# Four layer norms with an early half mean: squares summed under the last units, a new order in first units, and later tiles moved by 256 bytes

## What is computed

```
def layer_norm(x, g, b):
    mu = mean(x); var = mean(square(x - mu))
    return (x - mu) * rsqrt(var + 1e-5) * g + b

for i in range(2):
    h = layer_norm(ALPHA * h + mixer(h), ln_mix_g[i], ln_mix_b[i])
    h = layer_norm(ALPHA * h + square(relu(h @ w_up)) @ w_down, ln_mlp_g[i], ln_mlp_b[i])
```

## Time and profile before

| What | Value |
|---|---|
| runs | 1338.17, 1333.67, 1337.58 us; median 1337.58 |
| the profiled execution | 1333.9 us, its span from first to last instruction 1332.1 us |
| TensorE busy | 1283.2 us, 96% of the span |
| VectorE busy | 888.7 us, 67% |
| ScalarE busy | 642.5 us, 48% |
| mean granted TensorE clock | 0.989 |
| weights and other data read | 196.08 MB, 148 GB/s over the span |

### The profile page before, as it was taken

One profiled execution on the slowest core, in us unless ns is written; L12 is line 12 of the kernel. 1 busy time (PEld: TensorE's weight loads), 2 busy tenths in 40 slices (PEclk: granted clock), 3 DMA queues, 4 the chain that ended last, 5 costly groups with the idle time before them and its releaser, 6 DMA issues.

```text
span 1332.1 us, 25095 instructions
## 1 busy us (share of the span) xinstructions
PE 1283.2 (96%) x10634; PEld 1245.3 (93%) x10634; DVE 888.7 (67%) x1374; ACT 642.5 (48%) x834; POOL 46.3 (3%) x40
## 2 busy tenths in 40 slices
PE   9989999999987999999999999999999999999997
PEld 8868999999987999999999999899998989999997
DVE  6875764565568567646565459899766655899843
ACT  5464453443453335435435444554454454777631
POOL 0561000000000000000000000000000000000000
PEclk9999999999998999999999999999999999999999
DMA  9222255455331134554533543334454241454430
GB/s 358 97 107 95 98 190 202 175 189 189 130 127 64 64 127 156 192 190 163 204 111 128 189 163 129 144 138 168 149 187 168 94 154 64 158 185 173 177 128 32
DMA packets 28505, 198.41 MB, mean 149 GB/s; under 512 B 3440, under 2 KB 3952, under 8 KB 4736
## 3 DMA queue, kind: packets, MB, share of 16 engines
q1 hardware_dynamic: 27792, 195.83, 40.5%
q10 hardware_dynamic: 624, 1.31, 0.3%
HBM read 196.08 MB, written 1.05 MB: 148 GB/s over the span
## 4 chain that ended last, share of the span: by engine, by line
PE 79%; DVE 11%; ACT 4%; issue 2%; DMA 2%; POOL 2%; DVEq 0%; ACTq 0%
PE lin L462 23%; PE lin L464 23%; PE lin L463 23%; DVE wlo L1471 3%; PE lin L544 3%; PE att L537 2%; DVE conv L1950 2%; DMA raw<-units_dram 2%; ACT whi L1029 1%; PE lin L567 1%; POOL pr L447 1%; DVE qk L1812 1%; DVE z L1562 0%; POOL lg L447 0%; DVE h L1568 0%
## 5 line engine op out<-in xcount | busy, mean ns | idle before, releaser
L462 PE MATMUL lin<-xh,whi 128*128 128x256 f32 x1936 | 555.7, 287 | 3.9 <-DVE xl L1525 2.1
L1471 DVE TENSOR_TENSOR wlo<-raw,whi 128x2048 fp32r<-128x2048 f32 x179 | 409.6, 2291 | 212.3 <-ACT whi L1029 211.6
L463 PE MATMUL lin<-xl,whi 128*128 128x256 f32 x1936 | 549.8, 284 | 0.0
L464 PE MATMUL lin<-xh,wlo 128*128 128x256 f32 x1936 | 549.5, 284 | 0.0
L1029 ACT ACTIVATE whi<-raw 128x2048 fp32r<-128x2048 f32 x183 | 348.6, 1907 | 180.6 <-PE lin L464 167.3
L462 PEld LDWEIGHTS lin<-xh,whi 128*128 128x128 f32 x1936 | 373.5, 193 | 8.7 <-issue 5.5
L463 PEld LDWEIGHTS lin<-xl,whi 128*128 128x128 f32 x1936 | 373.6, 193 | 0.6 <-issue 0.5
L464 PEld LDWEIGHTS lin<-xh,wlo 128*128 128x128 f32 x1936 | 373.4, 193 | 0.0
L462 PE MATMUL lin<-fh,whi 128*128 128x256 f32 x512 | 143.4, 280 | 0.0
L463 PE MATMUL lin<-fl,whi 128*128 128x256 f32 x512 | 142.8, 279 | 0.0
L464 PE MATMUL lin<-fh,wlo 128*128 128x256 f32 x512 | 142.8, 279 | 0.0
(11 more groups left out here) (336 smaller groups left out, 1600.9 us busy)
## 6 DMA issues: line engine op xcount, KB each, us to landing
raw<-units_dram SPq DMA_DIRECT2D x183, 1024.0 KB, 4.8
h<-x_dram SPq DMA_DIRECT2D x1, 1024.0 KB, 6.9
memT<-mem_dram ACTq DMA_DIRECT2D x1, 1024.0 KB, 4.8
out_dram<-h SPq DMA_DIRECT2D x4, 256.0 KB, 2.0
consts<-consts_dram SPq DMA_DIRECT2D x1, 864.0 KB, 15.6
narrow_a<-narrow_a_dram SPq DMA_DIRECT2D x1, 544.0 KB, 8.7
vec<-vectors_dram SPq DMA_DIRECT2D x1, 245.5 KB, 17.8
posi<-pos_dram SPq DMA_DIRECT2D x1, 128.0 KB, 8.6
```

What stands on the lines that cost most here:

```text
L462: mm(out, w[0], a[0], start=first, stop=False)
L463: mm(out, w[0], a[1], start=False, stop=False)
L464: return mm(out, w[1], a[0], start=False, stop=last)
L1471: v.tensor_tensor(wlo[u % RING][:], raw[u % RING][:], whi[u % RING][:].bitcast(f32), ALU.subtract).then_inc(lo_ready, 1)
```

## The change

- **The early mean.** In the middle of unit 2 of 4 (narrow) or 4 of 8 (wide) TensorE multiplies the sum of the first four blocks by ones (`near_sum`, a job of its own). VectorE subtracts an eightfold share of that from all blocks (`near_shift`): from the two pairs that are done, from the two pairs that are still to come by way of the residual, and from zsum. From then on the blocks lie around a value near the mean.
- **Squares under the last units.** ScalarE squares each block as soon as it is done (`near_squares`), VectorE adds the squares up (`add_squares`), the last unit of a narrow group becomes two jobs of one block each. After the last block one tile of squares is left for TensorE to sum. The true variance is that sum less the square of the remaining mean: ScalarE squares the mean's row of one partition (shsq), TensorE adds it with a factor of -1 (a new constant, neg).
- **The norm.** VectorE waits for that square, centres two pairs, takes the reciprocal, and centres the other two, the third with a wait for its end. zsum is cleared after h.
- **`unit_first`** does the two products with xh of a pair first and the one with xl a pair later, at all eleven places.
- **Keep-warm matmuls**: in `norm` 2 instead of 4 ahead of `spread`; in `layer_norm` 1, 2 and 8 instead of 6, 4 and 11.
- **Loops.** The second half of the down projections is written out instead of looped.
- **Place.** An unused tile of 224 bytes per partition behind xl, and 8 more columns of constants, put consts 224 bytes and all tiles behind it 256 bytes higher.

```diff
+                def with_high(c):
+                    pe.wait_ge(split_hi, SPLIT[event] + c + 1)
+                    for m in range(2):
+                        for k in (2 * c, 2 * c + 1):
+                            w = tile(u, m * DB + k)
+                            mm(o[:, m, :], w[0], xh[:, k, :], start=m == k == 0, stop=False)
+                            mm(o[:, m, :], w[1], xh[:, k, :], start=False, stop=False)
...
+                with_high(0)
+                for c in range(1, 4):
+                    with_high(c)
+                    with_low(c - 1)
+                with_low(3).then_inc(job_done, 1)
...
+            def near_sum(ln):
+
+                pe.wait_ge(z_summed, SUMMED[ln] + 4)
+                mm(bank(JOB[ln + "_shift", 0])[:, 0, :], ones, zsum[:], start=True, stop=True).then_inc(job_done, 1)
...
             def norm(name, idle=6):
                 keep_warm(idle)
                 square_sum(name)
-                keep_warm(4)
+                keep_warm(2)
                 spread(name)
                 keep_warm(11)
...
                 mm(bank(JOB[name + "_mean", 0])[:, 0, :], ones, zsum[:], start=True, stop=True).then_inc(job_done, 1)
-                norm(name)
+                pe.wait_ge(near_added, ADDED[name] + 5)
+                o = bank(JOB[name + "_sq", 0])
+                token_sum(o, 0, squares_of[0][:, 0, :], True, False)
+                keep_warm(1)
+                pe.wait_ge(shift_squared, LN[name] + 1)
+                flat = o[:].rearrange("p a s -> p (a s)")
+                for t in range(2):
+                    last = mm(flat[:, t * P:t * P + 8], shsq[:, t * P:(t + 1) * P], const("neg")[0:1, :], start=False, stop=t == 1)
+                last.then_inc(job_done, 1)
+                keep_warm(2)
+                spread(name)
+                keep_warm(8)
...
             def layer_norm(name, event, bias):
-                squares(name, z, is_centered(name))
+
+                j = JOB[name + "_mean", 0]
+                filled(act, j)
+                f(shsq, lin[j % RING][0:1, 0, :], ACT.Square, scale=D ** -0.5).then_inc(shift_squared, 1)
...
+            def narrow_units(name, ln):
+
+                for i in range(4):
+                    high_part(U0[name] + i + AHEAD)
+                    if i == 3:
+                        near_squares(ln, is_shifted(ln, 0), (0, 1))
+                        near_squares(ln, is_shifted(ln, 1), (2, 3))
+                        near_squares(ln, lambda: evacuated(act, JOB[name, 2]), (4, 5))
+                near_squares(ln, lambda: evacuated(act, JOB[name, 3]), (6,))
+                near_squares(ln, lambda: evacuated(act, JOB[name, 3] + 1), (7,))
...
-                center(name, z, D)
-                inverse(name)
-                link(v.memset(zsum[:], 0.0))
-                is_centered(name)
+                j = JOB[name + "_mean", 0]
+                p = psum(j)
+                dve.wait_ge(shift_squared, LN[name] + 1)
+                for c in range(4):
+                    ins = v.scalar_tensor_tensor(out=two(z, c), in0=over(p[:, 0, :]), scalar=-1.0 / D, in1=two(z, c), op0=ALU.mult, op1=ALU.add)
+                    if c == 3:
+                        read_out(ins, j)
+                    elif c == 1:
+                        inverse(name)
+                    elif c == 2:
+                        link(ins)
+                evacuated(dve, j)
...
+            def near_shift(ln, src, alpha):
+
+
+                j = JOB[ln + "_shift", 0]
+                p = psum(j)
+                for n, c in enumerate((2, 3, 0, 1)):
+                    v.scalar_tensor_tensor(out=two(z, c), in0=over(p[:, 0, :]), scalar=-2.0 / D / (alpha if c >= 2 else 1.0),
+                                           in1=two(src if c >= 2 else z, c), op0=ALU.mult, op1=ALU.add).then_inc(shifted, 1)
+                read_out(v.scalar_tensor_tensor(out=zsum[:], in0=p[:, 0, :], scalar=-8.0 / D, in1=zsum[:], op0=ALU.mult, op1=ALU.add), j)
+                evacuated(dve, j)
+                dve.wait_ge(shifted, 4 * LN[ln] + 4)
...
                 for i in range(4):
                     low_part(U0[name] + i + AHEAD)
                     j = JOB[name, i]
...
+                    if i == 2:
+                        near_shift(ln, h, ALPHA)
+                    elif i == 3:
+                        add_squares(ln, 1, 2, sq[0][:], sq[1][:])
+                        add_squares(ln, 2, 3, sq[0][:], sq[2][:])
+                        add_squares(ln, 3, 3, sq[0][:, 0, :], sq[0][:, 1, :])
...
+                        for m in (6, 7):
+                            j = JOB[name, 3] + m - 6
+                            read_out(v.scalar_tensor_tensor(out=z[:, m, :], in0=z[:, m, :], scalar=ALPHA, in1=psum(j)[:, 0, :], op0=ALU.mult, op1=ALU.add), j)
+                            evacuated(dve, j)
+                            add_up(m, SUMMED[ln] + m + 1)
+                            add_squares(ln, 4 + m - 6, 4 + m - 6, sq[0][:, 0, :], sq[3][:, m - 6, :])
...
+                        for i in range(8):
+                            low_part(U0[dn] + i + AHEAD)
                             j = JOB[dn, i]
...
+                            if i == 4:
+                                near_shift(ln, z, 1.0)
+                            elif i == 6:
+                                add_squares(ln, 1, 2, sq[0][:], sq[1][:])
+                            elif i == 7:
+                                add_squares(ln, 2, 4, sq[0][:], sq[2][:])
+                                add_squares(ln, 3, 5, sq[0][:, 0, :], sq[0][:, 1, :])
+                                add_squares(ln, 4, 5, sq[0][:, 0, :], sq[3][:, 0, :])
+                            read_out(v.tensor_tensor(z[:, i, :], z[:, i, :], psum(j)[:, 0, :], ALU.add), j)
```

More of the change, by code:

```diff
@@ L98, in plan @@
         add("scores", p, banks=2)
-    units("ao", 4); norm("ln0", True)
+    narrow_units("ao", "ln0")
     for layer in range(2):
         for half in range(2):
-            units(f"up{layer}{half}", 8); units(f"dn{layer}{half}", 8)
+            units(f"up{layer}{half}", 8)
+            if half == 0:
+                units(f"dn{layer}0", 8)
+        for i in range(8):
+            if i == 4:
+                add(f"ln{2 * layer + 1}_shift")
+            add(f"dn{layer}1", i, f"dn{layer}1")
         norm(f"ln{2 * layer + 1}", True)
@@ L115, in plan @@
             add("gla_sq"); add("gla_rstd", 0); add("gla_rstd", 1)
-            units("go", 4); norm("ln2", True)
+            narrow_units("go", "ln2")
     norm("pre_mix")
@@ L320, in build @@
         SCALED = counts([(e, 3) for e in ("ln0", "ln1", "ln2", "ln3", "pre_mix", "mem", "pre_x", "pre_ffn")])
[L321 to L322 removed]
+        CENTERED = counts([("conv", 1)])
+        LN = {"ln0": 0, "ln1": 1, "ln2": 2, "ln3": 3}
+        SQUARED = counts([("pre_mix", 4), ("conv", 2), ("mem", 4),
                           ("post_mix", 4), ("pre_x", 4), ("post_x", 4), ("pre_ffn", 4), ("post_ffn", 4)])
[L325 removed]
+        PAIRS = {"conv": (0, 1), "mem": range(4), "post_mix": range(4),
                  "post_x": range(4), "post_ffn": range(4)}
@@ L330, in build @@
                                        "post_x", "pre_ffn", "post_ffn")])
-        SUMMED = {"ln0": 0, "ln1": 8, "ln2": 16, "ln3": 24}
+        SUMMED = {ln: 8 * i for ln, i in LN.items()}
+        NEAR = counts([("ln0", 5), ("ln1", 6), ("ln2", 5), ("ln3", 6)])
+        ADDED = {ln: 5 * i for ln, i in LN.items()}
         def per(n, g, step):
@@ L780, in mlp @@
                                 unit_up(U0[up] + i, JOB[up, i], g)
-                    with pe.Fori(0, 2) as g:
-                        for i in range(RING):
-                            unit_down(U0[dn] + i, JOB[dn, i], None if i else 8 * (2 * layer + half), g)
+                    if half == 0:
+                        with pe.Fori(0, 2) as g:
+                            for i in range(RING):
+                                unit_down(U0[dn] + i, JOB[dn, i], None if i else 16 * layer, g)
+                    else:
+                        for i in range(8):
+                            unit_down(U0[dn] + i, JOB[dn, i], None if i else 16 * layer + 8, ln=f"ln{2 * layer + 1}" if i == 4 else None)
                 layer_norm(f"ln{2 * layer + 1}")
```

118 lines of the change are left out of this document (85 added, 33 removed).

## The result

The changed kernel takes 1327.50 us, the median of 7 runs (1322.79 to 1329.98). The kernel before took 1333.71 beside it (7 runs, 1330.49 to 1338.17). The ratio is 0.9943 with a 95% interval of 0.9925 to 0.9960, so the change takes 6.2 us off by the medians and 7.6 by the ratio (5.3 to 10.0).

What follows compares the result with a forecast made beforehand. The prediction took TensorE to bound the kernel (79% of the last chain), gains coming where it waits for a short serial chain. 4.5+2.4+0.1-1.3 = 5.7 us less, from 1337.58 to 1331.9; range 1326.0 to 1337.6.

Steps and rivals of the forecast that it cites:

- the four S: Starts of the scaling in ln0 to ln3: forecast 0.0, 2.3, 0.3 and 1.9 us earlier, 4.5 in all.
- the first units: TensorE's units right behind ln0, ln1 and ln2: new product order gains 0.8 us each, 2.4 in all.
- the units elsewhere: The eight other units using the new product order: 0.1 us gained, ends 0 and 1.1.
- The clock: ln0 and ln2: TensorE's stall ahead of the mean loses the clock, 0.65 us each (0 to 1.3), 1.3 in all.
- M to S: Layer norms, end of the mean's matmul to start of scaling: 3.35 us, 3.62 in ln0, against 6.01 before in ln0.
- M: End of the mean's matmul: forecast 139.06 in ln0, 2.35 us later, and 331.11 in ln1, against 330.44.
- The late narrow sum: ln0 and ln2: VectorE's queue delays the last sum, so ln0's mean starts at 138.4 instead of 136.01; TensorE idles 2.4 us.
- The near sum: Extra mean matmul on TensorE mid-unit ahead of each layer norm: makes all that follows 0.53 us later.
- The rival that the clock stays down in all four norms: Half clock at each norm from the wait for the mean through the first unit; up to 1345.5 us; chance 0.10.
- Keep-warms: Two instead of four in the other norms gain nothing (0 to 0.1 us each).
- The place: Tiles 256 bytes higher: taken as 0, at most 5.6 us slower; as a rival 1337.5 us, chance 0.08.

Runs made afterwards that it cites:

- narrow_warm: Changed kernel with 14 instead of 5 keep-warm matmuls ahead of the mean in ln0 and ln2; run twice, 1327.02 and 1326.66 us.
- order_only: Kernel before, with only the new product order of the first units (`unit_first`); 1329.67 us, ratio 0.9975.
- warm_back: Changed kernel with the old keep-warms in two places: 11 instead of 8 ending a layer norm, 4 instead of 2 in other norms; 1327.61 us.
- place_only: Kernel before, with only the unused tile and 8 more columns of constants, so tiles lie 256 bytes higher; 1332.84 us, ratio 0.9996.
- late_low_warm: Changed kernel, VectorE's last narrow weight part moved behind the norm's last xl, 8 instead of 5 keep-warms ahead of ln0 and ln2 means; 1323.05 us.
- wide_only: Changed kernel with ln0, ln2 and the four units ahead of each done the old way; 1322.69 us, ratio 0.9914.
- late_both: late_low_warm with the writes of h and clearing of zsum in ln0 and ln2 moved behind the eight up units; 1320.81 us, ratio 0.9899.
- order_back: Changed kernel with the old product order in the first units; 1329.29 us, ratio 0.9959.

## Why the prediction was right, and where it was off

The forecast was 5.7 us less; 6.2 were measured. The median of 1327.50 lies in the range, 4.4 below the 1331.9 given. Most of that is the level: the 1337.58 of three runs that it started from came out at 1333.71 in seven, 3.9 lower, and the prediction had noted that its profiled execution lay 3.7 below the median.

That 5.7 comes so near 6.2 is in part luck, since the terms were off in both directions. Read from the marks, at full clock the four S come 5.7 earlier (4.5 forecast), the first units give 2.5 (2.4), ln3 gives 1.3 behind S (nothing was forecast) and the units elsewhere 0.5 (0.1): 10.0 for 7.0. The clock takes back 1.3 at each narrow norm that loses it (0.65 forecast), so 7.4 are left where both do. Each term follows.

**M to S.** Forecast 3.35, measured 3.25 in ln1, ln2 and ln3. Right, and for the reason given: VectorE alone sets S. In ln0 it was 4.36 and not 3.62; the root waited 0.56 for TensorE's small matmuls at half clock and the scaling 0.31 for the spread, a part of the clock's price that I had not put there. With the clock kept it is 3.53 (narrow_warm).

**M.** In ln0 it came at 139.07 (forecast 139.06), and that is luck: the mean started at 137.95 instead of 138.4, and its own pair of matmuls took 0.42 more at half clock (1.12 for 0.70), which I had not counted; in ln1 at 330.92 (331.11). The late narrow sum was foreseen, with its idle time of 2.4 (2.25 measured).

**The near sum.** Taken as 0.53, measured 0.43. By the rows above the unit's next matmul starts 0.25 behind the near sum (125.37 to 125.62) and the one behind that 0.30 later instead of 0.12. With it the four S come to 0.9 later, 2.5, 0.7 and 2.1 earlier (the table's T to S, less 0.43 each): 4.4 for the 4.5 of the sum. This match too is luck, since the later S of ln0 holds 1.25 of lost clock, which the sum has in a term of its own. At full clock ln0 is 0.4 earlier (T to S 7.99 in narrow_warm) and the four make 5.7: the near sum and the way from M to S were each 0.1 shorter than taken, at all four norms, and the last narrow sum was 0.2 earlier behind T.

**The first units.** 0.8 each was the term; 0.82, 0.83 and 0.81 came (T to U less T to S), and the first unit ends 8.09 behind S (8.05 forecast, 8.91 before). order_only has the same by itself. The other units look to be worth more than the 0.1 taken: 0.23 is seen behind ln3, and the profiled pair has some 0.5 outside the norms. The 3.3 of order_only fit that, but their interval, 1.3 to 5.3, also takes in 2.5.

**The clock.** Right in place and cause: the stalls ahead of the means of ln0 and ln2, shown by narrow_warm, which differs in nothing else, with the count of all profiles. Mis-sized: I took 0.65 each, from between 0 and 1.3, and it is 1.24 in ln0 and 1.3 in ln2. The step that failed was the middle of the range: the matmuls that it slows are the small ones of the chain itself, so nearly the whole price shows. What I did not foresee is that it is not lost in every execution (ln2 kept it in one profile of three), and that keeping it at both (narrow_warm) would raise the whole kernel's mean clock from 0.986 to 0.987 only. The rival that the clock stays down in all four norms is refuted: ln1 and ln3 are at 1.00 in the rows above, with fewer keep-warms than before.

The Trainium skill's rule in "TensorE: Matmul & The Clock Gate", section "A second HAM failure mode: psum-queue depth-cycling", would have short idles between groups of matmuls cost the clock; the trace does not agree for the gaps of ln1, the longest 0.75 us, at 1.00 throughout. The single stall of 2.25 us, which did cost the clock, is not what that section describes.

**Keep-warms.** Taken as nothing. Wrong at two places. Behind ln3 the row of 34 stood flush ahead of the square sums of the next norm. The step failed because I looked at the two keep-warms ahead of `spread` and not at the block behind it, whose end matters where another norm follows. It is worth 0.67, and with the 0.43 of the earlier start 1.1, a term of the sum that was missing: 1.3 of gain between S and U in ln3, with the 0.23 of the order. And at a narrow norm that lost the clock, the thinner block is worth 0.6 to 1.0, by warm_back.

**The place.** Nothing, as taken: place_only leaves no room for a loss of 5.6 (its interval ends at 1.2 slower).

**Still open.** Why late_low_warm and wide_only keep a mean clock of 0.990 and 0.991 and narrow_warm only 0.987, though its narrow norms are at full clock in both profiles. Each profile shows one execution, and the stretches at half clock between 360 and 430 us and behind 840 us differ from one to the next: those near 850 and near 1020 us are both missing in the profiles of the changed kernel, place_only and late_both, and both there in the other nine. A run that counts them over many executions was not tried.

## What to carry to other kernels

When a serial chain is shortened by doing its parts earlier, look at what they are queued behind on their engine: the early squares made the last sum 2 us late, and moving one weight part and the writes of h out of the way, with three keep-warms more, brought the median from 1327.50 to 1320.81, as much again as the change itself. But leaving the narrow norms as they were (wide_only) brought 4.8 of these 6.7 without any of that, and the two kernels' intervals overlap: where a chain is not shortened after all, the plain form is the first thing to try. A wait of 2 us on TensorE costs more than itself: measure the granted clock of the stretch behind it, and fill it or shorten it. And compare kernels at the same mean clock before ascribing a few us to an edit.

## What was not expected of the hardware

A stall of 2.25 us ahead of a small matmul, with ten keep-warm matmuls before it and a dense unit before those, was followed by 6.8 us at 0.50 in ln0, and by none in ln2 of the same execution, with a stall of 2.24. The same stalls in order_back and warm_back lost it in both norms. So a stall of the same length can cost the clock or not, and one profile does not settle whether an edit costs it. Nor had I expected that the clock kept at two places (narrow_warm) would be missed in the mean all the same.
